# Two products in place of three in the down projections: operand and rest side by side, 512 columns into both halves of a PSUM bank

## What is computed

```python
# first block, layers 0 and 1 (D_FF = 2816)
gate, val = jnp.split(u, 2, axis=-1)
return (jax.nn.silu(gate) * val) @ w_down          # (256, 2816) @ (2816, 1024)
...
x = x + conv_ffn(...)
# second block, layers 0 and 1 (D_FF_2 = 4096)
x = x + g2 * (jnp.square(jax.nn.relu(h2 @ w_ff1[l])) @ w_ff2[l])   # (256, 4096) @ (4096, 1024)
```

## Time and profile before

| | |
|---|---|
| times of three runs | 1320.43, 1320.58, 1322.57 us |
| median | 1320.58 us |
| the profiled execution | 1322.87 us, of which 1320.7 us from first to last instruction |
| TensorE busy, matmuls | 1287.2 us, 10934 matmul records |
| VectorE busy | 983.3 us |
| ScalarE busy | 740.2 us |
| GpSimd busy | 336.0 us |
| HBM traffic | 276.02 MB read, 210 GB/s over the span |

### The profile page before, as it was taken

The page is one execution under the profiler, slowest core; times in us unless marked ns, Lnnn a source line. Parts: engine busy times, 40 slices in busy tenths (PEclk is TensorE's granted clock), DMA queues, the critical chain, the costliest instruction groups (busy, mean ns, idle before and its releaser), DMA issues.

```text
span 1320.7 us, 25664 instructions
## 1 busy us (share of the span) xinstructions
PE 1287.2 (97%) x10934; PEld 1250.8 (95%) x10934; DVE 983.3 (74%) x1233; ACT 740.2 (56%) x956; POOL 336.0 (25%) x178
## 2 busy tenths in 40 slices
PE   8999999999999999999999999999999999999997
PEld 7889999999999999999999998999999999899997
DVE  5867899976677499997658786999865877644443
ACT  6657766655665466655555645544355565655432
POOL 6000255500000225540024002763001500177200
PEclk9999999999999999999999999999999999999999
DMA  8434687675654457776444546889934544455551
GB/s 300 144 123 170 261 309 259 246 266 197 224 185 151 155 186 285 304 272 235 138 165 163 182 174 221 291 316 347 378 133 161 175 175 162 164 195 197 200 196 37
DMA packets 41297, 278.72 MB, mean 211 GB/s; under 512 B 4704, under 2 KB 5216, under 8 KB 9824
## 3 DMA queue, kind: packets, MB, share of 16 engines
q1 hardware_dynamic: 33840, 226.15, 47.9%
q10 hardware_dynamic: 7344, 50.94, 10.7%
HBM read 276.02 MB, written 1.05 MB: 210 GB/s over the span
## 4 chain that ended last, share of the span: by engine, by line
PE 78%; DVE 14%; ACT 4%; issue 3%; DMA 1%; DVEq 0%; SPq 0%; ACTq 0%
PE bank L890 21%; PE bank L892 21%; PE bank L891 21%; DVE low L1648 6%; DVE adax L2024 2%; ACT high L1239 2%; PE bank L856 2%; PE bank L849 1%; PE bank L868 1%; PE bank L869 1%; PE bank L870 1%; PE bank L850 1%; DMA raw<-stream 1%; PE bank L948 1%; PE bank L1083 1%
## 5 line engine op out<-in xcount | busy, mean ns | idle before, releaser
L1648 DVE TENSOR_TENSOR low<-raw,high 128x2048 fp32r<-128x2048 f32 (+4 forms) x222 | 495.2, 2234 | 183.7 <-ACT high L1239 182.9
L890 PE MATMUL bank<-op_high,low 128*128 128x256 f32 (+1 forms) x1896 | 531.4, 280 | 6.3 <-DVE low L1648 6.3
L891 PE MATMUL bank<-op_low,high 128*128 128x256 f32 (+1 forms) x1896 | 524.1, 276 | 0.0
L892 PE MATMUL bank<-op_high,high 128*128 128x256 f32 (+1 forms) x1896 | 524.0, 276 | 0.0
L1239 ACT ACTIVATE high<-raw 128x2048 fp32r<-128x2048 f32 (+3 forms) x223 | 407.1, 1827 | 135.7 <-PE bank L892 122.8
L890 PEld LDWEIGHTS bank<-op_high,low 128*128 128x128 f32 (+1 forms) x1896 | 354.1, 187 | 12.6 <-DVE low L1648 9.4
L891 PEld LDWEIGHTS bank<-op_low,high 128*128 128x128 f32 (+1 forms) x1896 | 354.1, 187 | 2.6 <-issue 2.2
L892 PEld LDWEIGHTS bank<-op_high,high 128*128 128x128 f32 (+1 forms) x1896 | 353.9, 187 | 0.3
L890 PE MATMUL bank<-act_high,low 128*128 128x256 f32 x864 | 238.9, 276 | 0.7 <-DVE low L1648 0.7
L892 PE MATMUL bank<-act_high,high 128*128 128x256 f32 x864 | 238.5, 276 | 0.0
L891 PE MATMUL bank<-act_low,high 128*128 128x256 f32 x864 | 238.5, 276 | 0.0
(11 more groups left out here) (342 smaller groups left out, 1848.5 us busy)
## 6 DMA issues: line engine op xcount, KB each, us to landing
raw<-stream SPq DMA_DIRECT2D x197, 1024.0 KB, 5.0
adaw<-ada ACTq DMA_DIRECT2D x28, 1024.0 KB, 6.8
adax<-ada ACTq DMA_DIRECT2D x20, 1024.0 KB, 6.4
raw<-stream SPq DMA_DIRECT2D x10, 768.0 KB, 5.9
raw<-stream SPq DMA_DIRECT2D x10, 512.0 KB, 3.5
raw<-stream SPq DMA_DIRECT2D x2, 640.0 KB, 3.9
x<-xT SPq DMA_DIRECT2D x2, 512.0 KB, 4.4
out<-h SPq DMA_DIRECT2D x4, 256.0 KB, 2.8
```

What stands on the lines that cost most here:

```text
L890: pe.matmul(o, wl[:, w], oh[:, k, :], start=one, stop=False, skip_group_check=True)
L891: pe.matmul(o, wh[:, w], ol[:, k, :], start=False, stop=False, skip_group_check=True)
L892: mm = pe.matmul(o, wh[:, w], oh[:, k, :], start=False, stop=end, skip_group_check=True)
L1648: dve.tensor_tensor(low[m % SPLIT][:, at:w], raw[m % RAW][:, at:w], high[m % SPLIT][:, at:w], ALU.subtract).then_inc(S["low_ready"], 1)
```

## The change

For pairs 0 to 2 of the four projections (list `JOINT`, 42 chunks) the two products with the high weights become one: the high operand and its rest now are the two halves of one tile `act` (`AP`, `BP`; the two stood next to each other in the list of tiles already), and one product of 512 columns, read as 2 x 256, goes into both halves of a bank. The product of the low weights by the high operand (256 columns) follows into half 1, where the rest's product lies. Each output group then has a bank of its own, and VectorE adds the two halves of two banks to `x`: first half 1 of both, then, behind a wait for its own result, half 0 of both (`joint_to_x`).

```diff
@@ -47,6 +47,10 @@
                              for i in range(n)] + ["wo0_3", "wo1_3"]


+JOINT = [f"{tag}_{p}_{i}" for tag, n in (("down0", 3), ("down1", 3), ("fb0", 4), ("fb1", 4))
+         for p in range(3) for i in range(n)]
+
+
 def linear_chunks():


@@ -58,9 +62,10 @@
         ncols = len(cols)
         nb = max(1, ncols // 256) if not diag else 2
         halves = name in HALVES
-        apart = halves or ncols == 160
+        joint = name in JOINT
+        apart = halves or ncols == 160 or joint
         c.append(dict(name=name, src=src, rows=list(rows), cols=cols, first=first, last=last, tm=tm,
-                      diag=diag, op=op, banks=2 if apart else nb, apart=apart, halves=halves and last,
+                      diag=diag, op=op, banks=2 if apart else nb, apart=apart, joint=joint, halves=halves and last,
                       width=ncols * (1 if diag else len(rows))))

     def cols(a, n):
@@ -302,8 +307,8 @@

         ffn = ExitStack()
         f = lambda n, s, d=F32: sb(n, s, d, ffn)
-        AH = f("act_high", [P, 22, TOK], F32R)
-        AL = f("act_low", [P, 22, TOK], F32R)
+        AP = f("act", [P, 2, 22, TOK], F32R)
+        AH, AL = AP[:, 0, :, :], AP[:, 1, :, :]
         cg = [f(f"gate{i}", [P, 2, TOK]) for i in range(2)]
         cv = [f(f"val{i}", [P, 2, TOK]) for i in range(2)]
         ffn.close()
@@ -347,8 +352,8 @@

         ffn2 = ExitStack()
         f = lambda n, s, d=F32: sb(n, s, d, ffn2)
-        BH = f("act2_high", [P, 32, TOK], F32R)
-        BL = f("act2_low", [P, 32, TOK], F32R)
+        BP = f("act2", [P, 2, 32, TOK], F32R)
+        BH, BL = BP[:, 0, :, :], BP[:, 1, :, :]
         rl = [f(f"relu{i}", [P, 2, TOK]) for i in range(RELU)]
         adax = [f(f"adax{i}", [P, 2, D]) for i in range(2)]
         ffn2.close()
@@ -887,6 +892,12 @@
                         w = slice(i * ncols + parts[b][0], i * ncols + sum(parts[b]))
                         one = ch["first"] and (ch["diag"] or k == turns[0]) and (ch["apart"] or b % 2 == 0)
                         end = ch["last"] and (ch["diag"] or k == turns[-1])
+                        if ch["joint"]:
+                            pair = (BP if act == "B" else AP)[:, :, k, :]
+                            pe.matmul(ps[bank_of(ch, b)][:], wh[:, w], pair, start=one, stop=False, skip_group_check=True)
+                            mm = pe.matmul(ps[bank_of(ch, b)][:, 1, :], wl[:, w], oh[:, k, :], start=False, stop=end,
+                                           skip_group_check=True)
+                            continue
                         pe.matmul(o, wl[:, w], oh[:, k, :], start=one, stop=False, skip_group_check=True)
                         pe.matmul(o, wh[:, w], ol[:, k, :], start=False, stop=False, skip_group_check=True)
                         mm = pe.matmul(o, wh[:, w], oh[:, k, :], start=False, stop=end, skip_group_check=True)
@@ -1678,6 +1689,20 @@
                 else:
                     ins.then_inc(S["squares_added"], 1)

+            def joint_to_x(ch, p, gain=None):
+                for part in (1, 0):
+                    for i in range(2):
+                        k = 2 * p + i
+                        o = ps[bank_of(ch, i)][:, part, :]
+                        if gain is None:
+                            ins = dve.tensor_tensor(x[:, k, :], o, x[:, k, :], ALU.add)
+                        else:
+                            ins = dve.scalar_tensor_tensor(out=x[:, k, :], in0=o, scalar=gain[:, k:k + 1], in1=x[:, k, :],
+                                                           op0=ALU.mult, op1=ALU.add)
+                    if part:
+                        link(ins)
+                ins.then_inc(S["x_updated"], 1)
+
             def add_to_x(b, p, gain=None):
                 xp = x[:, 2 * p:2 * p + 2, :]
                 if gain is None:
@@ -1771,7 +1796,7 @@
                 elif name.startswith("odo"):
                     add_to_x(b, int(name[3]))
                 elif name.startswith("down") and ch["last"]:
-                    add_to_x(b, int(name.split("_")[1]))
+                    joint_to_x(ch, int(name.split("_")[1]))
                 elif name.startswith("up"):
                     l, j, v = int(name[2]), int(name[4:]), int(name[3] == "v")
                     dst = (cg, cv)[v][j % 2]
@@ -1822,7 +1847,7 @@
                     add_to_x(b, int(name[-1]), mod[:, l, 16:24])
                 elif name.startswith("fb") and ch["last"]:
                     l = int(name[2])
-                    add_to_x(b, int(name.split("_")[1]), mod[:, l, 40:48])
+                    joint_to_x(ch, int(name.split("_")[1]), mod[:, l, 40:48])

             def low_after(name):
                 if BY[name]["n"] not in BEFORE_NORM.values():
```

## The result

The changed kernel takes 1332.72 us (median of four runs, 1332.03 to 1333.16), the one before 1321.3 us (four runs, 1320.43 to 1322.57): a ratio of 1.0082, interval 1.0070 to 1.0094. It is slower by 11.4 us, where +3.2 us were forecast; the time lies above the range. It is what rival C gives with pair 3 in it (1332.2 us).

A forecast was written before the change was run, and what follows sets the result against it. The distance between TensorE's successive products was taken as the bound. 648 groups at 5.0 ns more gave +3.2 us, all else 0, on 1320.6: 1323.8 us; likeliest case 1322.2 to 1325.3, 8 in 10 range 1318.5 to 1329.5 us.

The forecast's parts named there:

- rival C: Four projections: changing lengths hold 256-column products at 117.8 ns, 353.4 ns per group; 1329.3 us, or 1332.2 with pair 3; chance 0.13.
- What bounds the kernel: In the four projections TensorE is busy throughout, so only the distance from one product to the next sets the time.
- The weight load, and no gap per product: TensorE in the projections: weight loads are hidden and time goes with the columns, so dropping a product saves nothing.
- rival B: TensorE's new groups: a fixed gap per product is saved, 220.0 + 113.3 = 333.3 ns, 4.3 us less, 1316.3 us; chance 0.12.
- The new group, 345 ns: Pairs 0 to 2: one long and one short product take 345 ns against 340.0, 648 times, +3.2 us.
- the upper end of my bounds, 347.2: Highest cost expected per new group: 229.2 ns for the long product plus 118 for the short one, +4.7 us.
- That lasted for five products: Argument against slow-paced groups: behind the twelve earlier long products, only five short ones stood at 118 ns.
- Pair 3 keeps its 113.3 ns: Pair 3 of the four projections, code untouched: its three products per group stay at 113.3 ns, no added time.
- the upper half of C: Pair 3's 648 products also stay at the slow pace, 2.9 us more, 1332.2 us; chance 0.07, left outside the range.
- Two runs of 256 cost nothing more: The long product's operand, read as two runs of 256 columns in place of one of 512, adds nothing.
- VectorE: Twelve longer additions, about 1.0 us more each, 12 to 13 us in all, hidden behind 4.8 us of cover.
- Banks at nothing: Each pair takes two banks of six in place of one; no claim waits, so 0 us.

The follow-up runs named there:

- the kernel before without step products: The kernel before the change without the seven small float32 products placed ahead of seven chunks (IN_STEP): 1326.82 us, ratio 1.0032.

## Why the prediction was right or wrong, point by point

- **What bounds the kernel**: right. The distance between products decided the time of the four stages (11.4 us more there, 11.4 measured), and no new wait shows.
- **The weight load, and no gap per product**: right. 648 loads fewer gained nothing, and no long product of these runs came under 225 ns (twice 113.3 is 226.7), where rival B needed 220.0. So no order of long and short products that was tried beat the 340.0 ns of three short ones, and the experiments point to no version faster than the one before. By the rule of the Trainium skill, page "TensorE: Matmul & The Clock Gate", section "Wait — 56ns, not 53.3ns?", it would be 215.8 ns; the traces don't agree.
- **The new group, 345 ns: wrong, and this is the step that failed.** It measured 353.3 ns; 648 x 8.3 = 5.4 us of the miss of 8.9 (1332.7 against 1323.8). I took the distance of the first long product behind a short one and of the short ones behind long ones, as events. They were the way into a lasting state. The 0.227 is right for a product that finds TensorE in step (1231.07), but from the second group on none does, and the upper end of my bounds, 347.2, held only 229.2 for a long product where 235 stand. The 229.2 came from twelve in a row; no row showed a single one with short ones on both sides, so the upper end should have been the slow pace for all 768 columns, 353.4: rival C's own number.
- **"That lasted for five products"**, my reason against C: rightly counted in the earlier trace rows and wrongly used. It holds behind twelve long products in a row, and the new order has no two in a row. And the stretch of the earlier trace rows, of which I took 45 products, is longer: the slow pace lasts there from 112.51 to 133.47 us, 178 distances, and no 512-column product stands among them. One of its lines over 112.6 to 133.3 us:

```profile
L890 PE MATMUL bank<-mix_high,low 128*128 128x256 f32 x48 | 13.5, 281 | 0.0
```

  So the trace before the change already showed that the slow pace can last. The last experiments show that long products in a row, one pair being enough, can be followed by the fast one. That the twelve ended the five in this way isn't shown: behind a pair one short product is slow, behind the twelve five.
- **Pair 3 keeps its 113.3 ns**: wrong, 117.8, 2.9 us. Its code is untouched, but the state it starts in isn't. I had it as the upper half of C and cut the range below it. The last 0.7 us of the miss are the base: with a fourth run the kernel before has a median of 1321.3 in place of 1320.6 us.
- **Two runs of 256 cost nothing more**: right (one contiguous run gave the same distances).
- **VectorE**: right. Its busy time rose by 10.3 us, somewhat less than the 12 to 13 reckoned, and it is hidden. The four additions of line 1700 in `fb0`, the low part behind them, and ScalarE at the end of TensorE's chunk, in order of time:

```profile
920.50 1.78 DVE L1700 SCALAR_TENSOR_TENSOR x<-bank,mod,x 128x256 f32<-128x256 f32 x4
...
922.58 2.29 DVE L1659 TENSOR_TENSOR low<-raw,high 128x2048 fp32r<-128x2048 f32 x1 [0.30 <-ACT high L1250]
```

```profile
929.58 1.92 ACT L1250 ACTIVATE high<-raw 128x2048 fp32r<-128x2048 f32 x1 [3.40 <-PE bank L898]
```

  The additions take 1.78 us where the earlier trace rows had 0.87, 0.9 more as reckoned. The low part is done at 924.87 us, TensorE's chunk at 929.58: 4.7 us of cover are left.
- **Banks at nothing**: right (0.5 us of idle time ahead of 648 long products; the three short ones in the new banks ran at 1320.92 us).
- **The chances**: slower was given 0.49, and rightly led, but mostly for a price at each change of length, 3.2 us in all, not for the lasting pace that cost 11.4. C had 0.13, too little: the slow pace was a thing the trace had shown, over 45 products in the earlier trace rows, and the change mixes lengths, of which no steady row existed. The range needed all of C.

**Open**: what in TensorE the two paces are. Nor is it settled why two long products in a row bring the fast one back and one with four short ones behind doesn't, why five short ones stay slow behind the twelve of the earlier trace rows, or why these were 229.2 ns apart and 87 in a row 233.4.

## What to carry to other kernels

Before a longer product is put among short ones, look at the pace that the short ones have, in start-to-start distances, and at whether the trace shows that very mixture in a long stretch; a dozen products in another order are a transient, not a price. A stage's pace can be inherited: when one stage changes, read the distances in the untouched stage behind it too. Where two paces are known, take the slow one as the bound.

## What the runs showed of the hardware that was not expected

- The pace of 256-column fp32r products is a state, 113.3 or 117.8 ns at a granted clock of 1.00, and it lasts: in the kernel before without step products a stage stayed at 117.8 for all of its 768 products. One small float32 product ends it.
- It can be read without distances, by the mean record: 276 ns at the fast pace, 281 at the slow one, and 0.39 against 0.40 us for 512 columns.
- In these runs one 512-column product among 256-column ones leaves TensorE at the slow pace, also with four short ones between two long ones; then it costs 235 ns. Two in a row are followed by the fast pace, at 226 + 236 + 118 + 113 ns for two long and two short ones. Long ones alone settle at a mean of 233.4 ns.
